# Trunk layer on one core: band scores in row halves, another order of the band steps

## What is computed

```python
h = rms_norm(x, mix_norm[l])
proj = h @ w_in[l]
c_q, c_kv, k_pe, q_s, k_s, v_s = jnp.split(proj, IN_SPLIT_POINTS, axis=-1)
y_mla = mla_attention(c_q, c_kv, k_pe, ...) @ w_o_mla[l]
y_swa = swa_attention(q_s, k_s, v_s, rel_bias, swa_sinks[l]) @ w_o_swa[l]
g_mla, g_swa = jnp.split(jax.nn.sigmoid(h @ w_gate[l]), N_BRANCHES, axis=-1)
x = x + (g_mla * y_mla + g_swa * y_swa) @ w_out[l]
...
# in swa_attention: chunks of 64 queries see 128 keys (their own chunk and the one before)
logits = jnp.einsum('bcqhgd,bckhd->bchgqk', q, kb) * (SWA_HEAD_DIM ** -0.5) + rel_bias
m = jnp.maximum(jnp.max(logits, axis=-1, keepdims=True), sink)
p = jnp.exp(logits - m)
denom = jnp.sum(p, axis=-1, keepdims=True) + jnp.exp(sink - m)
o = jnp.einsum('bchgqk,bckhd->bcqhgd', p / denom, vb)
```

## Time and profile before

| | us |
|---|---|
| median of 3 runs | 1121.86 |
| the profiled execution | 1122.17 |
| its span in the profile | 1120.4 |
| PE busy | 1109.7 |
| DVE busy | 567.0 |
| ACT busy | 419.0 |
| POOL busy | 149.1 |

### The profile page before, as it was taken

One profiled execution on the slowest core, in us unless ns is written; L12 is line 12 of the kernel. 1 busy time (PEld: TensorE's weight loads), 2 busy tenths in 40 slices (PEclk: granted clock), 3 DMA queues, 4 the chain that ended last, 5 costly groups with the idle time before them and its releaser, 6 DMA issues.

```text
span 1120.4 us, 14760 instructions
## 1 busy us (share of the span) xinstructions
PE 1109.7 (99%) x5194; PEld 908.4 (81%) x5194; DVE 567.0 (51%) x852; ACT 419.0 (37%) x719; POOL 149.1 (13%) x119
## 2 busy tenths in 40 slices
PE   9999999999999999999999999999999999999996
PEld 7888888888888888777777788888888888888896
DVE  6644344433455536876565554546443444434454
ACT  7322222222335325776544533334221233212253
POOL 0211011100114102320000002231110011101122
PEclk9999999999999999999999999999999999999999
DMA  7235222332224221051321232322233222323222
GB/s 269 87 100 122 95 94 94 97 105 98 94 70 132 98 94 61 11 149 50 118 72 62 73 97 94 95 94 94 94 98 105 97 94 94 94 95 103 88 71 76
DMA packets 35262, 107.21 MB, mean 96 GB/s; under 512 B 4224, under 2 KB 7968, under 8 KB 35216
## 3 DMA queue, kind: packets, MB, share of 16 engines
q1 hardware_dynamic: 34464, 105.43, 29.1%
q0 software_dynamic: 192, 0.78, 0.6%
q10 hardware_dynamic: 560, 0.41, 0.1%
HBM read 101.76 MB, written 2.88 MB: 93 GB/s over the span
## 4 chain that ended last, share of the span: by engine, by line
PE 97%; DVE 1%; ACT 1%; issue 0%; POOL 0%; DMA 0%; SPq 0%; DVEq 0%; POOLq 0%; ACTq 0%
PE bank L1352 29%; PE bank L1354 29%; PE bank L1353 29%; PE bank L1502 2%; PE bank L1532 1%; PE bank L1697 1%; PE bank L1699 1%; PE bank L1698 1%; PE bank L1557 1%; PE bank L1492 1%; PE bank L1542 1%; DMA x<-in_x_t 0%; PE bank L1464 0%; PE bank L1459 0%; PE bank L1469 0%
## 5 line engine op out<-in xcount | busy, mean ns | idle before, releaser
L617 ACT ACTIVATE w_hi<-staged 128x1024 fp32r<-128x1024 f32 x182 | 193.0, 1061 | 543.5 <-PE bank L1354 543.4
L1352 PE MATMUL bank<-xg_hi,w_hi 128*128 128x512 f32 x1000 | 395.0, 395 | 0.0
L1354 PE MATMUL bank<-xg_hi,w_lo 128*128 128x512 f32 x1000 | 389.5, 389 | 0.0
L1353 PE MATMUL bank<-xg_lo,w_hi 128*128 128x512 f32 x1000 | 389.3, 389 | 0.0
L922 DVE TENSOR_TENSOR w_lo<-staged,w_hi 128x1024 fp32r<-128x1024 f32 x182 | 225.5, 1239 | 107.9 <-ACT w_hi L617 107.8
L1352 PEld LDWEIGHTS bank<-xg_hi,w_hi 128*128 128x128 f32 x1000 | 187.7, 188 | 44.0 <-issue 6.1
L1354 PEld LDWEIGHTS bank<-xg_hi,w_lo 128*128 128x128 f32 x1000 | 187.7, 188 | 39.8
L1353 PEld LDWEIGHTS bank<-xg_lo,w_hi 128*128 128x128 f32 x1000 | 187.8, 188 | 38.6 <-issue 0.7
L511 POOL TENSOR_TENSOR h_lo<-hid,h_hi 128x512 f32 x44 | 70.6, 1604 | 590.7 <-ACT h_hi L640 534.9
L1352 PE MATMUL bank<-h_hi,w_hi 128*128 128x512 f32 x304 | 118.4, 389 | 0.2 <-POOL h_lo L511 0.2
L1353 PE MATMUL bank<-h_lo,w_hi 128*128 128x512 f32 x304 | 118.3, 389 | 0.0
(11 more groups left out here) (182 smaller groups left out, 1062.6 us busy)
## 6 DMA issues: line engine op xcount, KB each, us to landing
staged<-in_ffn_w SPq DMA_DIRECT2D x118, 512.0 KB, 3.3
staged<-in_w_gate SPq DMA_DIRECT2D x16, 512.0 KB, 3.7
staged<-in_w_in SPq DMA_DIRECT2D x15, 512.0 KB, 3.3
staged<-in_ffn_w SPq DMA_DIRECT2D x16, 384.0 KB, 3.1
staged<-in_w_ob SPq DMA_DIRECT2D x8, 512.0 KB, 3.4
staged<-in_w_out SPq DMA_DIRECT2D x8, 512.0 KB, 3.4
x<-in_x_t SPq DMA_DIRECT2D x8, 256.0 KB, 5.1
staged<-in_w_oa SPq DMA_DIRECT2D x4, 512.0 KB, 3.3
```

The lines of the kernel that those rows point to most:

```text
L617: nc.scalar.activation(w_hi[:, u % SPLIT, :], staged[:, u % STAGED, :], ACT.Copy).then_inc(hi_done, 1)
L1352: nc.tensor.matmul(o, wh, hi, start=start, stop=False)
L1353: nc.tensor.matmul(o, wh, lo, start=False, stop=False)
L1354: return nc.tensor.matmul(o, wl, hi, start=False, stop=stop)
```

## The change

- **Band scores.** `ks` has one column block in which kv 0 lies in rows 0 to 63 and kv 1 in rows 64 to 127. `band_scores(c)` makes all scores of a chunk at once: for each of the four pairs two matmuls with 64 rows and 128 columns, kv 0 into bank 4 and kv 1 into bank 5. A band step n is now one kv of a chunk with all four pairs, where it was two pairs with both kv. Bias, sinks and the order of the transposed tiles follow.
- **Values.** `swa_values(c)` makes two matmuls over 512 columns per chunk, where there were four over 256.
- **Order on PE.** Scores come once in two steps, behind the transposes of the even step; chunk 0's come behind the first piece of the plan.
- **Order on DVE.** In the band steps `split_next` stands ahead of the scores, and both score sets of a chunk run one after the other in the even step.
- **Order on ACT.** In even band steps `split_next` stands ahead of `read_transposed`; in odd ones `exponentials(n+2)` stands ahead of `split_next`.
- **Order on POOL.** The pieces of a slot (additions of squares, the rotary key, a root) stand one `normalise` later.
- **The plan.** Five gates instead of three lie in the first 17 slots, ten instead of twelve are spread over the MLA steps; `uk` is two and two tiles with gate 2 between; two more splits have a place of their own. `rope_2` is loaded into `root_sq`. One more slot in `gates` and `summed`.

```diff
-EARLY_GATES = 3
+EARLY_GATES = 5
...
+            [("kpe", 0, 1), ("uk", 0, 0), ("uk", 1, 0)],
+            [("sum", 0, "q"), ("rest", 4, "q")] + halves("gate", 2),
+            [("uk", 2, 0), ("split", 0, "uq"), ("uk", 3, 0)],
+            [("split", 3, "gate"), ("root", 0, "q"), ("uq", 0, 0), ("gate", 3, 0)],
...
-                if w == UNIT_AT["gate", 1]:
-                    sp.wait_ge(lat_ready, 2)
-                    sp.dma_start(lat[:, 0, :], rope_2).then_inc(rope_in, 16)
+                if w == UNIT_AT["uk", 0]:
+                    sp.wait_ge(lat_step, 3)
+                    sp.dma_start(root_sq[:, :], rope_2).then_inc(rope_in, 16)
...
             for n in range(STEPS):
                 if n + 1 < W_STEPS:
                     normalise(n + 1)
-                for piece in PLAN[n + 1]:
+                for piece in PLAN[n]:
                     filler(*piece)
...
             for n in range(STEPS):
+                early = n % 2 == 0 and n < W_STEPS
+                if early:
+                    split_next(PLAN[n])
                 read_transposed(n)
-                split_next(PLAN[n])
+                if n % 2 == 1 and n + 2 < W_STEPS:
+                    exponentials(n + 2)
+                if not early:
+                    split_next(PLAN[n])
                 if n >= 1:
                     read_output(n - 1)
-                if n + 2 < STEPS:
+                if (n % 2 == 0 or n + 2 >= W_STEPS) and n + 2 < STEPS:
                     exponentials(n + 2)
...
-                if n + 2 < STEPS:
+                if n + 2 < W_STEPS:
+                    split_next(PLAN[n])
+                    if n % 2 == 0:
+                        scores(n + 2)
+                        scores(n + 3)
+                elif n + 2 < STEPS:
                     scores(n + 2)
-                split_next(PLAN[n])
...
+            def band_scores(c):
+
+                if c == 0:
+                    pe.wait_ge(vband_ready, 2)
+                    pe.wait_ge(ks_clear, 1)
+                    pe.wait_ge(grp_read, g + G_QS + SG)
+                else:
+                    pe.wait_ge(exp_done, 2 * c)
+                for pair in range(SG // 2):
+                    for kv in range(SKV):
+                        rows = slice(kv * SD, (kv + 1) * SD)
+                        last = nc.tensor.matmul(bank[S_BANK + kv][:, pair * BAND:(pair + 1) * BAND],
+                                                qs[rows, pair, c, :, :].rearrange("p a b -> p (a b)"),
+                                                ks[rows, c * CHUNK:c * CHUNK + BAND], start=True, stop=True)
+                        if pair == SG // 2 - 1:
+                            last.then_inc(s_ready, 1)
...
-                if n + 2 < STEPS:
+                if W_STEPS <= n + 2 < STEPS:
                     scores(n + 2)
                 transposes(n)
+                if n + 2 < W_STEPS and n % 2 == 0:
+                    band_scores(n // 2 + 1)
```

More of the change, by code:

```diff
@@ L75, in fillers @@
 def fillers():
[L77 to L83, removed]
-            [("round", 0, "kv"), ("rest", 3, "q"), ("latent", 4, 1)],
[L85 to L92, removed]
+    plan = [halves("latent", 0) + [("latent", 1, 0)],
+            [("latent", 1, 1)],
+            halves("latent", 2),
+            [("sum", 0, "kv"), ("latent", 3, 0)],
+            [("kpe", 0, 0), ("root", 0, "kv"), ("rest", 2, "q"), ("latent", 3, 1)],
+            [("newton", 0, "kv"), ("gate", 0, 0)],
+            [("scale", 0, "kv"), ("gate", 0, 1), ("latent", 4, 0)],
+            [("round", 0, "kv"), ("rest", 3, "q"), ("latent", 4, 1)],
+            [("rest", 0, "kv")] + halves("gate", 1),
+            [("kpe", 0, 1), ("uk", 0, 0), ("uk", 1, 0)],
+            [("sum", 0, "q"), ("rest", 4, "q")] + halves("gate", 2),
+            [("uk", 2, 0), ("split", 0, "uq"), ("uk", 3, 0)],
+            [("split", 3, "gate"), ("root", 0, "q"), ("uq", 0, 0), ("gate", 3, 0)],
+            [("uq", 1, 0), ("split", 4, "gate"), ("gate", 3, 1)],
+            halves("gate", 4),
+            [("uv", 0, 0)],
             [("uv", 1, 0), ("uv", 2, 0)],
@@ L250, in gate_at @@
         def gate_at(t):
-            return gates[:, GATE_SLOTS[t] // 2, GATE_SLOTS[t] % 2, :]
+            return gates[:, GATE_SLOTS[t], :]
         def sum_at(k, low):
-            slot = GATE_SLOTS[2 * k + low]
-            return summed[:, slot // 2, slot % 2, :]
+            return summed[:, GATE_SLOTS[2 * k + low], :]
         def group_bank(n):
@@ L575, in _ @@
                     normalise(n + 1)
-                for piece in PLAN[n + 1]:
+                for piece in PLAN[n]:
                     filler(*piece)
+            for piece in PLAN[STEPS]:
+                filler(*piece)
             pool.wait_ge(*own)
@@ L1529, in transposes, with swa_values @@
                 for t in range(4 if n < W_STEPS else m_step(n)[1] + 1):
-                    to = (t % 2) * 2 + t // 2 if n < W_STEPS else t
-                    last = nc.tensor.transpose(b[:, to * P:(to + 1) * P], probs[:, n % 2, t * P:(t + 1) * P], idn[:, :])
+                    last = nc.tensor.transpose(b[:, t * P:(t + 1) * P], probs[:, n % 2, t * P:(t + 1) * P], idn[:, :])
                 last.then_inc(t_ready, 1)
-            def swa_values(n):
-                half = n % 2
-                pe.wait_ge(t_read, n + 1)
-                if n >= 2:
-                    pe.wait_ge(o_read, n // 2)
-                for h in range(SKV):
-                    rows = slice(h * SD, (h + 1) * SD)
-                    last = nc.tensor.matmul(bank[O_BANK][rows, half * 2 * P:(half + 1) * 2 * P], vband[:, n // 2, rows],
-                                            probs_t[:, n % 2, h * 2 * P:(h + 1) * 2 * P], start=True, stop=True)
-                last.then_inc(pv_done, 1)
+            def swa_values(c):
+                pe.wait_ge(t_read, 2 * c + 2)
+                if c >= 1:
+                    pe.wait_ge(o_read, c)
+                for kv in range(SKV):
+                    rows = slice(kv * SD, (kv + 1) * SD)
+                    nc.tensor.matmul(bank[O_BANK][rows, :], vband[:, c, rows], probs_t[:, kv, :],
+                                     start=True, stop=True).then_inc(pv_done, 1)
             def mla_values(n):
@@ L1635, in _ @@
             filler(*PLAN[0][0])
-            scores(1)
+            band_scores(0)
             for piece in PLAN[0][1:]:
```

79 lines of the change are left out of this document (28 added, 51 removed).

## The result

| | us |
|---|---|
| before, median (1121.82 to 1122.21) | 1121.92 |
| after, median (1134.14 to 1134.90) | 1134.55 |
| after / before, 95% interval | 1.0112 (1.0094 to 1.0129) |
| profiled execution after: own time, span | 1134.14, 1132.4 |
| predicted, range | 1128.7, 1124 to 1133 |

What follows compares the result with a forecast made beforehand. PE, busy 99% of the span, was taken to bound the kernel. 1122.17 - 5.2 (scores) - 0.7 (POOL's wait) + 12.8 (new waits) = 1129.1 us, or 1128.7 against the median; range 1124 to 1133.

Steps and rivals of the forecast that it cites:

- the clock: Rival: PE's clock falls to 1.2 GHz in wait (1), one stretch costing 2 us; 1130.7, up to 1133; chance 0.15.
- wait (1): At the sum for q (slot 10), PE waits for the chain of ACT and DVE: 5.1 us.
- (3): At unit uq 0, whose split starts only when uk 3 is done, PE waits 2.8 us, at least 2.1.
- (4): At gate 3, whose split stands behind uk 3's copies and exponentials(13), PE waits 1.8 us, up to 2.1.
- (2): At gate 2, which needs the bank of uk 0 that ACT copies late, PE waits 0.7 us.
- (5): At gate 4, which goes into uq 0's slot after uq 1, PE waits 0.5 us.
- (6): At transposes(0), PE waits for two score sets, the reciprocal and POOL: 0.3 us, to 0.7.
- (7): At transposes(6), DVE has newton's three operations between the score sets and normalise(6): 0.9 us, 0 to 1.3.
- (8): Small waits at normalise(8) and at lat_lo for uk 0: 0.5 us.
- Serial rows: Rival: row halves of the scores run one after the other, 7.0 us more stream; 1132.3; chance 0.13.
- Shorter waits: Rival: PE comes 3 us late at wait (1) and (7), (8) vanish; 1124.5 (1122 to 1126); chance 0.11.
- faster: Rival: the other engines' chains end ahead of PE, every wait but 0.5 us goes; 1116.5; chance 0.09.

Runs made afterwards that it cites:

- busy_two: The changed kernel with 11 and 8 useless matmuls filling PE's waits ahead of the uq 0 and gate 3 products only: 1133.05 us.
- uk_in_one: The changed kernel with all four uk products ahead of gate 2 and both uq products ahead of gate 3 in the plan: 1126.6 us.
- busy_one: The changed kernel with 20 useless matmuls of 512 columns filling PE's wait ahead of the sum for q: 1130.0 us.
- old_plan: The changed kernel with the plan and the three early gates of before, row halves and new engine orders kept: 1130.1 us.
- both_first: kpe_first with ACT's copies of uk 0 and uk 1 also moved ahead of exponentials(10): 1123.35 us.
- pool_behind: The kernel before with only POOL's pieces moved behind the next multiplication of the softmax: 1121.64 us against 1122.29, ratio 0.9993.
- kpe_first: uk_in_one with DVE's read of the rotary key moved ahead of the two score sets in step 8: 1126.5 us.
- replan_in_turn: replan with a chunk's eight band score matmuls issued key group after key group, not by turns: 1121.15 us.
- replan: The changed kernel with another plan for slots 2 to 17: 1118.96 us against 1122.22 of the kernel before, ratio 0.9971.
- replan_2: replan with the rotary product moved to slot 11, the sum for q to slot 9, two splits spread: 1118.67 us, ratio 0.9968 to before.

## Why the prediction was wrong

**The step that failed is the clock**, by what it was left out of. The sum let PE come back from every wait at the speed at which it went in; the case in which it doesn't stood as a rival with 0.15, for wait (1) alone, at 2 us. The runs show it each time: all three traces in which PE waits 4.9 us (after, busy_two, uk_in_one) have a low stretch there, as had the one idle start in the trace of before. busy_one prices the clock at 4.5 us. It came twice: in wait (1), 2.2 in eleven products and some 0.4 in the sum for q, a little more than the rival's 2; and 1.6 behind (3) and (4), idle times of 2.65 and 1.90 us with 2.3 us of work between them, when the prediction called the 5 us wait the only one long enough to compare with an idle start. old_plan and both_first have low stretches behind waits of 1.1 to 1.7 us. With both low stretches of after the same sum gives 1128.7 + 4.5 = 1133.2; 0.6 more are the scores and 0.4 the waits, below, and 0.3 is left. The Trainium skill ("TensorE: Matmul & The Clock Gate", Part 1) states that an idle engine is throttled to 1.2 GHz and released by sustained work. busy_one and busy_two agree in kind: 0.43 us a product behind the unfilled wait, 0.23 behind the filled one.

**Scores**: 4.6 for 5.2, inside its bounds. Side by side was right; what was short is mostly the cost next to the values, where a chunk takes 1.09 and not 0.88 + 0.15, and 0.1 for each of chunks 0 and 1. **Values, moved work, rope load**: 0.0, no wait shows there. **POOL's wait**: 0.7, right, by pool_behind.

**The waits**, forecast and measured by starts: (1) 5.1, 5.14, and 0.0 for 0.2 at `band_scores(5)`; (2) 0.7, 0.5 (busy_one, where the clock doesn't hide it: a pause of 0.27 and its restart); (3) 2.8, 2.88; (4) 1.8, 2.06; (5) 0.5, 0.80; (6) 0.3, 0.47; (7) 0.9, 0.80; (8) 0.5, 0.52. In all 12.8 and 13.2. (1) was called the least certain and is exact, in part by luck: counted from the start of `band_scores(5)` at 479.61, PE's side took 6.7 us for the 6.4 of the sum (it has the wait at lat_lo in it) and the other side 11.8 for 11.5, and the two misses cancel. That the chain was the one described is shown by kpe_first, where the sum's wait falls by 3.4, the two score sets' 3.45, and by both_first. Of the short ones (4), (5) and (6) are 0.2 to 0.3 too low. By starts a wait is 0.16 to 0.26 longer than its column of idle time (0.80 for 0.64 at step 6); that this is why they came out low isn't shown.

**The rivals.** Serial rows: no, and the price, 7.0, was too high by 2.6 (4.4 in replan_in_turn). Shorter waits, faster: no; the decision at wait (1) to (5) against 5.9 went as (3) and (4) foretold, with 11.4, and the faster case is real only with another plan (replan, replan_2). The clock: yes, at twice its price of 2, so that even this rival's time, 1130.7 and up to 1133, was too low. No wait shows in the MLA steps, as stated.

## What to carry to other kernels

Work out a wait of the engine that bounds the kernel in two terms: its length, and what the engine's clock costs behind it (1.6 to 2.6 us a time here). Don't count on a wait being too short for it: here 1.1 to 1.7 us had it behind them in some places and not in others. Look for it in a busy table of short stretches, since a slice of the page is 28 us here and shows 9 even with a low stretch of 3.4 us in it (old_plan, both_first). Where a wait can't be removed, useless matmuls in it can be worth more than they look (4.5 us here for 20 of them). A gain on that engine is only as good as the order of work of the others: the same change of the scores gave 12.6 us more or 3.6 us less by the plan alone. If a wait has several ends that are released one behind the other, moving one of them moves the wait.

## What the runs showed of the hardware

- PE's granted clock fell to 0.50 (1.2 GHz) by the end of a wait of 4.9 us (after, busy_two, uk_in_one) and of two, 1.5 and 3.7 us, close together (kpe_first), for 6.8 us each time. It fell for 3.4 us behind waits of 3.0, 1.1 and 1.7 us in old_plan, of 1.5 and 0.2 us in both_first, and of 2.65 and 1.9 us in after, 0.2 to 1.5 us after PE was busy again. It didn't fall behind 2.65 and 1.9 us in busy_one, 1.46 in replan or another wait of 1.1 in old_plan. So the length of a wait doesn't tell it alone.
- Matmuls on the two row halves overlap when issued by turns (1.09 us for 16 records in replan) and hardly when issued half after half (1.64 in replan_in_turn).
- In replan DVE's minimum of 128x4 (`nmax`, 484.92) took 0.92 us while POOL's addition of 1.28 us ran (from 484.53); the next one, without it, took 0.16. Such a stretch was missing from the expectation of replan.
